# The end of a two-block transformer kernel: VectorE sums the last squares, two refinement steps for three, and the last rows leave in three pieces

## The reference

```python
def rmsnorm_2(x, w):
    xf = x.astype(jnp.float32)
    y = xf * lax.rsqrt(jnp.mean(xf * xf, axis=-1, keepdims=True) + EPS)
    return (y * w.astype(jnp.float32)).astype(x.dtype)

def swiglu(h, w_gate, w_up, w_down):
    return (jax.nn.silu(h @ w_gate) * (h @ w_up)) @ w_down
...
        h = h + swiglu(rmsnorm_2(h, norm_ffn[layer]), w_gate[layer], w_up[layer], w_down[layer])
    return rmsnorm_2(h, final_norm)
```

## Time and profile before

| | |
|---|---|
| median of 3 runs | 865.42 us (865.23 to 865.64) |
| the profiled execution, its own time | 865.03 us |
| its span | 863.2 us |
| granted TensorE clock, mean | 0.999 |
| TensorE busy | 854.1 us, 99% |
| VectorE busy | 566.5 us, 66% |
| ScalarE busy | 503.9 us, 58% |
| GpSimd busy | 124.3 us, 14% |
| HBM read, written | 144.32 MB, 1.05 MB |

### The profile page before, as it was taken

The page is one execution under the profiler, slowest core; times in us unless marked ns, Lnnn a source line. Parts: engine busy times, 40 slices in busy tenths (PEclk is TensorE's granted clock), DMA queues, the critical chain, the costliest instruction groups (busy, mean ns, idle before and its releaser), DMA issues.

```text
span 863.2 us, 12059 instructions
## 1 busy us (share of the span) xinstructions
PE 854.1 (99%) x4420; PEld 700.9 (81%) x4420; DVE 566.5 (66%) x1000; ACT 503.9 (58%) x901; POOL 124.3 (14%) x100
## 2 busy tenths in 40 slices
PE   9999999999999999999999999999999999999996
PEld 6877888778888888888888888888888888888885
DVE  6866866678776897755555446576897755555444
ACT  6668466765877874644444334777874644444332
POOL 0122054110153330000000000153230000000001
PEclk9999999999999999999999999999999999999999
DMA  9813554445444346655555555444246655565531
GB/s 315 288 57 106 189 198 142 145 149 174 152 142 147 100 145 219 217 186 177 178 193 196 195 194 171 151 147 147 98 147 219 213 176 177 192 195 184 192 112 49
DMA packets 94765, 146.14 MB, mean 169 GB/s; under 512 B 6516, under 2 KB 54900, under 8 KB 94708
## 3 DMA queue, kind: packets, MB, share of 16 engines
q1 hardware_dynamic: 92820, 139.52, 48.7%
q0 software_dynamic: 1296, 4.72, 1.6%
q10 hardware_dynamic: 592, 1.14, 0.4%
HBM read 144.32 MB, written 1.05 MB: 168 GB/s over the span
## 4 chain that ended last, share of the span: by engine, by line
PE 98%; DMA 1%; DVE 0%; issue 0%; SPq 0%; POOL 0%; ACT 0%; POOLq 0%; DVEq 0%
PE bank L1210 83%; PE bank L1145 7%; PE bank L1359 2%; PE bank L1287 1%; PE bank L1265 1%; PE bank L1262 1%; PE bank L1290 1%; DMA raw<-in_w_in_a 1%; PE bank L1349 0%; PE bank L1366 0%; PE bank L1327 0%; DVE lo L1719 0%; POOL scaled L1647 0%; PE bank L1308 0%; PE bank L1331 0%
## 5 line engine op out<-in xcount | busy, mean ns | idle before, releaser
L1044 DVE TENSOR_TENSOR lo<-raw,hi 128x1024 fp32r<-128x1024 f32 (+1 forms) x244 | 299.4, 1256 | 97.4 <-ACT hi L1380 95.1
L1380 ACT ACTIVATE hi<-raw 128x1024 fp32r<-128x1024 f32 (+1 forms) x260 | 266.9, 1059 | 106.2 <-PE bank L1210 101.9
L1210 PE MATMUL bank<-hi,xT_hi 128*128 128x512 f32 (+2 forms) x736 | 289.7, 394 | 0.3 <-DVE lo L1719 0.2
L1210 PE MATMUL bank<-hi,xT_lo 128*128 128x512 f32 (+2 forms) x736 | 282.6, 384 | 0.0
L1210 PE MATMUL bank<-lo,xT_hi 128*128 128x512 f32 (+2 forms) x736 | 281.7, 383 | 0.0
L1210 PEld LDWEIGHTS bank<-hi,xT_hi 128*128 128x128 f32 x736 | 138.3, 188 | 30.6 <-issue 4.3
L1210 PEld LDWEIGHTS bank<-hi,xT_lo 128*128 128x128 f32 x736 | 138.2, 188 | 28.1
L1210 PEld LDWEIGHTS bank<-lo,xT_hi 128*128 128x128 f32 x736 | 138.6, 188 | 24.7
L1210 PE MATMUL bank<-hi,hT 128*128 128x512 f32 x348 | 108.3, 390 | 0.0
L1210 PEld LDWEIGHTS bank<-hi,hT 128*128 128x128 f32 x348 | 65.3, 188 | 13.5
L1210 PE MATMUL bank<-lo,hT 128*128 128x512 f32 x174 | 67.7, 389 | 0.0
(11 more groups left out here) (259 smaller groups left out, 933.3 us busy)
## 6 DMA issues: line engine op xcount, KB each, us to landing
raw<-in_w_in SPq DMA_DIRECT2D x26, 1024.0 KB, 5.0
raw<-in_w_gate SPq DMA_DIRECT2D x44, 512.0 KB, 3.7
raw<-in_w_up SPq DMA_DIRECT2D x44, 512.0 KB, 4.7
raw<-in_w_down SPq DMA_DIRECT2D x22, 1024.0 KB, 4.8
raw<-in_w_out SPq DMA_DIRECT2D x20, 1024.0 KB, 5.0
raw<-in_w_in_b SPq DMA_DIRECT2D x10, 1024.0 KB, 5.0
raw<-in_w_in_a SPq DMA_DIRECT2D x7, 1024.0 KB, 7.3
raw<-in_w_in_a SPq DMA_DIRECT2D x4, 256.0 KB, 4.7
```

What stands on the lines that cost most here:

```text
L1044: return engine.tensor_tensor(lo[r][:, cols], raw[c.i % RAW][:, cols], hi[r][:, cols].bitcast(F32), ALU.subtract)
L1210: last = nc.tensor.matmul(bank[:, 0:wd], still[a], mv[r][:, off:off + wd], start=c.first and i == 0 and j == 0, stop=(c.last or c.closes a ...
L1380: nc.scalar.activation(hi[c.i % SPLIT][:, cols], raw[c.i % RAW][:, cols], ACT.Copy)\
```

## The change

The squares of the last tails are taken by VectorE, in one instruction each that multiplies, reduces and adds to an initial value; the part sums are gone, and the mean square adds only the sum over the first half. The order of steps is add q=0, square q=0, add q=1, square q=1. The refinement for the last norm (both halves of the rows) has two chained steps behind the power and one small product, by -0.5, that doesn't need it. ScalarE scales its columns of the last rows in two pieces of 256; SP sends the first of them, ScalarE the second, SP the upper half as before. One column `halved` is new in SBUF, and is placed ahead of `totals` and of the large tiles behind it.

```diff
-        tails = [sc.step("tail_added", q=q, bank=ending.tails[q], of=ending, before=early) for q in range(2)]
+        tails = []
+        part = None
         for q in range(2):
-            sc.step("square", n=1, m=1, q=q, added=tails[q])
-        part = sc.step("part_sum", of=sc.count["square"] - 2)
-        part = sc.step("part_sum", of=sc.count["square"] - 1, before=part)
+            tails.append(sc.step("tail_added", q=q, bank=ending.tails[q], of=ending, before=early))
+            part = sc.step("tail_square", q=q, added=tails[q], before=part)
...
+    halved = keep("halved", [P, 1])
...
+            sp.wait_ge(sem["result", "scalar"], 3)
+            sp.dma_start(t["out"][0, P:S, 0:256], result[:, 1, 0:256]).then_inc(out_done[0], 16)
             sp.wait_ge(sem["result", "vector"], 1)
             sp.dma_start(t["out"][0, P:S, 512:D], result[:, 1, 512:D]).then_inc(out_done[0], 16)
-            sp.wait_ge(out_done[0], 48)
+            sp.wait_ge(out_done[0], 64)
...
-                if s.q is not None:
-                    square_sum(h[:, 1, TAIL[s.q]], sumsq[:, 3 + s.q:4 + s.q], s)
-                    continue
...
-                for n in range(2 - s.m):
-                    c = slice(n * 512, (n + 1) * 512)
+                for n in range(2):
+                    cw = 256 if s.m else 512
+                    c = slice(n * cw, (n + 1) * cw)
...
-                    act.wait_ge(sem["result", "scalar"], 3)
-                    act.dma_start(t["out"][0, P:S, 0:512], result[:, 1, 0:512]).then_inc(out_done[1], 16)
+                    act.wait_ge(sem["result", "scalar"], 4)
+                    act.dma_start(t["out"][0, P:S, 256:512], result[:, 1, 256:512]).then_inc(out_done[1], 16)
...
-                        done(stt(ms, sumsq[:, 4:5], 1.0 / D, newt[:, 1, 0:1], ALU.mult, ALU.add), s)
+                        done(stt(ms, sumsq[:, 2:3], 1.0 / D, sumsq[:, 4:5], ALU.mult, ALU.add), s)
...
-            elif s.kind == "part_sum":
-                dve.wait_ge(sem["square", "scalar"], s.of)
-                if s.before is None:
-                    done(ts(newt[:, 1, 0:1], sumsq[:, 2:3], 1.0 / D, EPS, ALU.mult, ALU.add), s)
-                else:
+            elif s.kind == "tail_square":
+                ended(dve, s.added, "vector")
+                if s.before is not None:
                     ended(dve, s.before, "vector")
-                    done(stt(newt[:, 1, 0:1], sumsq[:, 3:4], 1.0 / D, newt[:, 1, 0:1], ALU.mult, ALU.add), s)
+                x = h[:, 1, TAIL[s.q]]
+                done(nc.vector.tensor_tensor_reduce(
+                    scaled[:, 1, TAIL[s.q]], x, x, 1.0 / D, sumsq[:, 3:4] if s.q else EPS, ALU.mult, ALU.add,
+                    sumsq[:, 3 + s.q:4 + s.q]), s)
...
-                ended(dve, s.before, "gpsimd")
                 _, ms, rs, y = norm_parts(s)
                 if s.what == "out":
-                    chained(stt(y, rs, ms, rs, ALU.mult, ALU.mult))
-                else:
-                    chained(tt(y, rs, rs, ALU.mult))
-                    chained(tt(y, y, ms, ALU.mult))
+
+                    ended(dve, s.before, "vector")
+                    chained(ts(halved[:, :], ms, -0.5, None, ALU.mult))
+                    ended(dve, s.before, "gpsimd")
+                    chained(stt(y, rs, halved[:, 0:1], rs, ALU.mult, ALU.mult))
+                    done(stt(rs, y, 1.5, rs, ALU.add, ALU.mult), s)
+                    continue
```

More of the change, by code:

```diff
@@ L822 @@
     "decay": ("tensor", "scalar"), "weigh": ("vector",), "diag": ("tensor",), "off": ("tensor",),
-    "join": ("vector",), "ysquare": ("scalar",), "ynorm": ("vector",), "final": ("vector",), "scaled": ("vector",), "part_sum": ("vector",), "tail_added": ("vector",), "pool_scaled": ("gpsimd",),
+    "join": ("vector",), "ysquare": ("scalar",), "ynorm": ("vector",), "final": ("vector",), "scaled": ("vector",), "tail_square": ("vector",), "tail_added": ("vector",), "pool_scaled": ("gpsimd",),
     "result": ("vector", "scalar"),
@@ L1404, in square_sum @@
                 ended(act, junked[-1], "scalar")
-            done(nc.scalar.activation(junk[:, 0:x.shape[-1]], x, ACT.Square, accum_out=out), s)
+            done(nc.scalar.activation(junk[:, :], x, ACT.Square, accum_out=out), s)
             junked.append(s)
@@ L1895, in _ @@
             elif s.kind == "newton":
-                ended(dve, s.before, "gpsimd")
                 _, ms, rs, y = norm_parts(s)
                 if s.what == "out":
-                    chained(stt(y, rs, ms, rs, ALU.mult, ALU.mult))
-                else:
-                    chained(tt(y, rs, rs, ALU.mult))
-                    chained(tt(y, y, ms, ALU.mult))
+                    ended(dve, s.before, "vector")
[4 more added lines that the diff above has]
+                    continue
+                ended(dve, s.before, "gpsimd")
+                chained(tt(y, rs, rs, ALU.mult))
+                chained(tt(y, y, ms, ALU.mult))
                 chained(ts(y, y, -0.5, 1.5, ALU.mult, ALU.add))
```

## The result

The changed kernel takes 868.97 us, the median of 6 runs (868.62 to 869.3); the kernel before takes 865.53 in 6 runs beside them (865.23 to 865.83). The ratio is 1.0038, with an interval of 1.0028 to 1.0047. It is slower by 3.4 us, where 0.36 us were forecast, and lies outside the forecast's range of 864.8 to 866.2. The profiled execution took 868.62 us with a span of 866.8, against 865.03 and 863.2: 3.6 us to account for.

A forecast was written before the change was run, and what follows sets the result against it. TensorE carries 98% of the span, so only the serial tail after its last matmul could move: squares +0.67, refinement -0.19, three pieces -0.12, sum +0.36 us, giving 865.8 us on the median; range 864.8 to 866.2.

The forecast's parts named there:

- the third rival: Matmuls in the body: the new column shifts later tiles by 64 bytes; over 1.7 us from 0.4 ns each; 8%.
- the disturbance of the first square: Last rows' tail: VectorE's square of q=0 waits for GpSimd's multiply of h and gains; mean square 0.67 us later.
- the refinement: Last norm, after GpSimd's power: three VectorE steps become two, -0.19 us; the product by -0.5 costs nothing.
- three pieces: Output of the last rows: the first piece's data flows sooner, so the end comes 0.12 us earlier; bounds -0.25 to +0.13.
- The prediction's other sum, +0.08: Output of the last rows: with a fixed 2.0 us per DMA the end follows the last issue alone, costing 0.08 us.
- The sum of the tail: After TensorE's last matmul: squares +0.67, refinement -0.19, output in pieces -0.12, together +0.36 us.
- No disturbance: First square in the tail: GpSimd does not delay it, so -0.43 us in all, 865.0 us; chance 15%.
- Slow accumulating form: Both VectorE squares in the tail: each takes a further 0.27 us, +0.90 in all, 866.3 us; chance 7%.

The follow-up runs named there:

- all_but_place: The whole change against the kernel before, but with the column halved in unused room of newt, so later tiles keep their old places; 866.53 us, ratio 1.0008.
- two_steps: The kernel before with the two-step refinement alone, the product by -0.5 in a free column of newt; 865.45 us, ratio 0.9997.
- three_pieces: The kernel before with only the last rows sent in three pieces; 865.77 us, ratio 1.0002.
- xT_64: The kernel before with xT moved by 64 bytes, oT, raw, hi and lo by 128, hT in place; 870.86 us in the one run left.

## Why the prediction was wrong

- **Wrong: the body.** The sum has no term for it ("the change does not touch the body of the program, so only what follows TensorE's last matmul can move"), and the step that put it at nothing is the third rival's price: "Nothing in the trace has matmuls of one shape differ by where their operand lies, so it is small". The rival had the mechanism (a new column moves every tile behind it by 64 bytes) and the sign, with 5% on the slow side and a threshold of 0.4 ns on all 4420 matmuls. It was 6 to 7 ns on 522 of them: 3.1 us. The sentence is also wrong as a reading. All matmuls of 128x512 with hi or lo moving stand at distance 0 in the trace of before, so their likeness was no evidence, and those of 128x272, which stand at four distances, do differ, by up to 10 ns. The range left the case out.
- **Right: the disturbance of the first square.** Forecast 0.67 later for the mean square; with the places undone it starts 1.98 after TensorE's end, and was 1.29: 0.69. The first square was on record for 1.22 (forecast 1.27), ending 0.28 after GpSimd. That the sum fits so well is in part luck: the square with both inputs in SBUF is 0.42 and not 0.47 and its read 0.08 and not 0.14, but the mean square starts 0.12 after the read's end and not 0.03.
- **Right in kind, too large: the refinement.** From the start of the first step to the end of the last it was 0.61, and is 0.41, as forecast (-0.19), and the power takes 0.55. But the first step used to start 0.03 after the power's end and now starts 0.11 after it (862.54 against 861.88 + 0.55 in the changed kernel, and the same in all_but_place and two_steps). It waits for two semaphores now, GpSimd's and that of the product by -0.5, which is the likely reason; no run takes this apart. That is 0.08 where the sum had nothing, and the part is worth 0.12.
- **Right: three pieces**, -0.12 forecast. From the end of the refinement to the span's end it is 864.62 - 860.80 = 3.82 in all_but_place and 3.83 in three_pieces, in place of 3.94. SP issued at 861.37 and 861.75, 0.38 apart where 0.41 was taken. The last issue came later than before and the end sooner, so the end didn't hang on the last issue alone. The prediction's other sum, +0.08 from a fixed cost per DMA, has the wrong sign here. The Trainium skill (DMA: Bandwidth & Descriptors, Anatomy of one DMA) gives that cost for DMAs that GpSimd issues; these are issued by SP and ScalarE.
- **The sum of the tail** was +0.36; all_but_place shows 0.69 - 0.12 - 0.13 = +0.44, which is 7.11 - 6.67, and 0.57 in the medians. Without the new column the forecast would have been off by 0.1 to 0.2 us.
- **The other rivals fell.** No disturbance: 1.22 on record. Slow accumulating form: 0.42 for the undisturbed square. The Trainium skill (Vector Engine (DVE) Microarchitecture Reference, Points that are easy to get wrong) has the halved throughput for the scalar-tensor-tensor form; carried over to the multiply-and-reduce, as the prediction did, it does not hold here, and the measurement decides.

## What to carry to other kernels

An edit that adds a buffer is two edits: compare the addresses of all later tiles, and if any is an operand of many matmuls, put the new buffer last or into unused room, then measure the padding alone. "All matmuls of this shape take the same" says nothing on their places as long as they all have the same place; look for a shape whose offsets vary. Before a VectorE instruction with two SBUF inputs is put on the last chain, look at what GpSimd runs at that moment: here 0.8 us of GpSimd's 1.27 were added to a square of 0.42. A gain of 0.1 to 0.3 us that is seen in a timeline can be real and still be out of reach of the medians; read it as a distance between two events of one trace, to 0.01 us, and read the same distance in kernels that did not change there. Where a step is given a second thing to wait for, look whether its start moves, even if both are there in time.

## What was not expected of the hardware

A matmul of 128x512 f32 is paced by how far its tile at rest and the moving tile lie from each other within 256 bytes: 389 to 390 ns with distance 0, 395 to 397 with hT 32, 64 or 128 behind, 394 and 389 with 192 behind. All together at another place: 389 to 390. Other shapes have other sizes. Those of 272 columns with lo moving are at 282 to 292 before, by their distance. Those of 256 columns are, by the tile's view, at 283 before, and at 276 in the changed kernel, with the 64 bytes that cost the others 6 ns:

```profile
L1190 PE MATMUL bank<-hi,hT x8: 277/283/283, 854.9 to 856.3; 128*128 128x256 f32 x8
```

```profile
L1193 PE MATMUL bank<-hi,hT x8: 276/276/281, 858.1 to 859.3; 128*128 128x256 f32 x8
```

With hT 32 or 128 bytes off they are at 280 to 282, and with 192 at 279 to 280; the 48 with xT in xT_64 are at 276. What in the chip does this, a shared path of the two reads or something else, no run here shows.
